# 18 of 22 MLP up units as Strassen's seven half-size products, the first conv tap on ScalarE

## The chip, the core and the metric

The kernel runs on one core of one Trainium2 chip. TensorE (PE) multiplies, VectorE (DVE), ScalarE (ACT) and GpSimd (POOL) work on tiles in SBUF, DVE and ACT also on PSUM, and SyncE (SP) issues the loads. The metric is the device time of one execution in microseconds; lower is better.

## The reference

Two layers of a decoder trunk over 512 tokens of width 1024, all in f32. Each layer has a token mixer, a cross-attention and a gated MLP, each between two RMS norms. The change is in the MLP alone:

```python
def conv_ffn(h, w_up, conv_w, conv_b, w_down):
    u = h @ w_up
    a, b = u[..., :D_FF], u[..., D_FF:]
    a = lax.conv_general_dilated(a, conv_w[:, None, :].astype(a.dtype), window_strides=(1,),
                                 padding=[(CONV_WIDTH - 1, 0)], dimension_numbers=('NWC', 'WIO', 'NWC'),
                                 feature_group_count=D_FF) + conv_b
    return (jax.nn.gelu(a) * b) @ w_down
```

with `D_FF` = 2816 and a convolution over three tokens, causal, channel by channel.

## The kernel before

**Precision.** Every large product runs in three passes on `float32r` operands: an f32 value is split into a high part (a copy to `float32r`) and a low part (the value less the high part), and the helper `three` issues low x high, high x low and high x high into one PSUM bank. Activations stand as `a_hi` and `a_lo`, 128 partitions x 8 chunks of the width x 512 tokens.

**Weights as a stream of units.** A layer reads 70 units of 1 MB. The up projection is units 36 to 57 (`U_UP` = 36), 22 of them, each 1024 x 256 columns: even ones for the value `a`, odd ones for the gate `b`. A unit is loaded by SP into one of two places of `raw`; ACT makes its high part in two halves of 128x1024 (L937, in `cast_halves`), POOL its low part in two halves (L795, `low_half`), and both stand in rings of two places, `w_hi` and `w_lo`. Unit u may be cast when an earlier unit has been used by PE (`unit_used`), and the low part waits for the high part.

**The up projection on PE.** The first pair of units (36 and 37) runs in halves of 256 tokens, from its own tiles `up_hi` and `up_lo`, between the transposes that still make `a_hi` and `a_lo`. From unit 38 on `cols_gemm` takes each unit in two column blocks of 128: for each 8 chunks x 3 matmuls with 512 tokens as the moving side, so 48 matmuls a unit, into two banks. Eight banks hold two pairs.

**Behind it.** With f one of 22 column blocks of 128 (`NF` = 22), DVE multiplies a bank by the third tap (`tensor_scalar`, L1687) and adds the two shifted taps (`scalar_tensor_tensor`, L1688 and L1689) into `conv`; ACT takes gelu of it into `gel` (L1244); DVE multiplies `gel` with the gate's bank into `gT` (`gate`, L1676). `gT` is then split for the down projection: high by ACT (`g_parts`), low by DVE (`g_rest`, L1670). Three of these splits stand within the up projection, the others behind it.

**Order.** Every engine runs its instructions in the order in which the code issues them, with semaphores between the engines. The order is written out by hand, one block for each engine; nothing is moved by a scheduler.

## Time and profile before

| | us |
|---|---|
| median of three runs (1682.21 to 1682.44) | 1682.44 |
| span of the profiled execution, first to last instruction | 1680.4 |
| PE busy | 1666.1 |
| POOL busy | 841.7 |
| ACT busy | 725.6 |
| DVE busy | 655.7 |

The page gives the profiled execution's span and no other time of it; what lies around the span is the difference to the runs, 2.0 us. Engines work side by side, so busy times don't add up. An instruction's duration runs from its start to its end; neighbours on an engine can overlap by some tens of nanoseconds, and a matmul's duration is longer than the distance to the next one. In a row, `[2.53 <-PE banks L1732]` is the engine's idle time before the instruction, and what ended it.

### The profile page before, as it was taken

What the parts mean: (1) busy time and instruction counts of PE and PEld (TensorE: products, weight loads), DVE (VectorE), ACT (ScalarE), POOL (GpSimd) and SP (SyncE); (2) the same over time, 40 slices, a digit from 0 to 9 for tenths busy, and PEclk for the clock granted to TensorE, in tenths of its full rate; (3) what the DMA queues carried; (4) which work ended last, traced back from release to release, by engine and by line L of the source; (5) the groups of instructions that cost most, each with busy time, mean ns of one, the idle gap of its engine ahead of it and who ended that gap; (6) DMA issues with size and microseconds to landing.
All of it is one profiled execution on the core that took longest, in us unless ns stands there. A gap on an engine that the chain in (4) does not pass through costs nothing.

```text
span 1680.4 us, 23253 instructions
## 1 busy us (share of the span) xinstructions
PE 1666.1 (99%) x9217; PEld 1366.6 (81%) x9217; DVE 655.7 (39%) x1423; ACT 725.6 (43%) x1386; POOL 841.7 (50%) x553
## 2 busy tenths in 40 slices
PE   9999999999999999999999999999999999999998
PEld 7888776888898888888888887768888988888886
DVE  3454665163272222311233456652442622232113
ACT  6326777363361222232362367764543522222322
POOL 4447667463443444445623567665634344443552
PEclk9999999999999999999999999999999999999999
DMA  6234111242232223232323340122413223332322
GB/s 227 76 96 137 51 27 52 80 146 75 64 99 96 85 95 100 76 125 100 110 93 100 93 139 27 26 53 87 163 50 109 81 75 101 100 101 75 106 95 75
DMA packets 101191, 154.15 MB, mean 92 GB/s; under 512 B 4396, under 2 KB 76380, under 8 KB 101084
## 3 DMA queue, kind: packets, MB, share of 16 engines
q1 hardware_dynamic: 98572, 147.16, 26.9%
q10 hardware_dynamic: 2512, 5.51, 0.9%
...
## 4 chain that ended last, share of the span: by engine, by line
PE 95%; ACT 1%; issue 1%; DVE 1%; POOL 1%; DVEq 0%; ACTq 0%; POOLq 0%
PE banks L1730 27%; PE banks L1732 27%; PE banks L1731 27%; PE banks L2045 4%; PE banks L2098 4%; PE banks L2074 4%; PE banks L1858 1%; PE banks L1774 1%; DVE proj L1559 1%; PE banks L2094 0%; PE banks L2242 0%; PE banks L1762 0%; POOL w_lo L795 0%; ACT w_hi L937 0%; ACT rows L906 0%
## 5 line engine op out<-in xcount | busy, mean ns | idle before, releaser
L795 POOL TENSOR_TENSOR w_lo<-raw,w_hi 128x1024 fp32r<-128x1024 f32 (+2 forms) x262 | 629.1, 2421 | 656.2 <-ACT w_hi L937 643.5
L937 ACT ACTIVATE w_hi<-raw 128x1024 fp32r<-128x1024 f32 (+2 forms) x264 | 259.8, 1028 | 643.4 <-PE banks L1732 635.5
L1730 PE MATMUL banks<-w_hi,a_lo 128*128 128x512 f32 (+1 forms) x864 | 332.5, 385 | 0.1
L1732 PE MATMUL banks<-w_hi,a_hi 128*128 128x512 f32 (+1 forms) x864 | 330.1, 382 | 0.0
L1731 PE MATMUL banks<-w_lo,a_hi 128*128 128x512 f32 (+1 forms) x864 | 330.0, 382 | 0.0
L1730 PE MATMUL banks<-a_hi,w_lo 128*128 128x512 f32 x768 | 299.6, 390 | 0.0
L1732 PE MATMUL banks<-a_hi,w_hi 128*128 128x512 f32 x768 | 298.9, 389 | 0.0
L1731 PE MATMUL banks<-a_lo,w_hi 128*128 128x512 f32 x768 | 298.8, 389 | 0.0
L1730 PEld LDWEIGHTS banks<-w_hi,a_lo 128*128 128x128 f32 x864 | 162.3, 188 | 32.8 <-issue 1.7
L1732 PEld LDWEIGHTS banks<-w_hi,a_hi 128*128 128x128 f32 x864 | 162.2, 188 | 31.3
L1731 PEld LDWEIGHTS banks<-w_lo,a_hi 128*128 128x128 f32 x864 | 162.3, 188 | 30.6
L1732 PEld LDWEIGHTS banks<-a_hi,w_hi 128*128 128x128 f32 x768 | 144.1, 188 | 30.0
L1731 PEld LDWEIGHTS banks<-a_lo,w_hi 128*128 128x128 f32 x768 | 144.2, 188 | 29.8
L1730 PEld LDWEIGHTS banks<-a_hi,w_lo 128*128 128x128 f32 x768 | 144.2, 188 | 29.3
L1687 DVE TENSOR_SCALAR conv<-banks,vecs 128x512 f32<-128x512 f32 x44 | 33.0, 749 | 224.8 <-PE banks L1732 224.8
L1545 DVE CUSTOM_DVE_ANT_0 banks<-banks,causal 128x128 f32<-128x128 f32 (+3 forms) x160 | 75.5, 512 | 40.2 <-PE banks L2045 40.2
L1670 DVE TENSOR_TENSOR a_lo<-gT,a_hi 128x1024 fp32r<-128x1024 f32 x18 | 28.6, 1592 | 153.3 <-ACT a_hi L1237 153.3
L805 POOL TENSOR_SCALAR proj<-proj,rden,gates 128x128 f32<-128x128 f32 (+3 forms) x128 | 76.4, 608 | 22.9 <-DVE rden L1563 22.5
L1093 ACT ACTIVATE proj<-banks,neg_max 128x128 f32<-128x128 f32 (+3 forms) x144 | 74.6, 526 | 7.3 <-DVE neg_max L1545 7.3
L2098 PE MATMUL banks<-probT,proj 128*64 128x128 f32 x960 | 73.6, 283 | 0.2
L2074 PEld LDWEIGHTS banks<-ident,proj 128*128 128x128 f32 x440 | 46.7, 140 | 32.8 <-issue 28.7
L2074 PE MATMUL banks<-ident,proj 128*128 128x128 f32 x440 | 67.8, 284 | 0.0
...
## 6 DMA issues: line engine op xcount, KB each, us to landing
raw<-in_ffn_w_up SPq DMA_DIRECT2D x44, 1024.0 KB, 5.1
raw<-in_ffn_w_down SPq DMA_DIRECT2D x20, 1024.0 KB, 4.9
raw<-in_w_in SPq DMA_DIRECT2D x19, 1024.0 KB, 5.1
raw<-in_x_wk SPq DMA_DIRECT2D x8, 1024.0 KB, 5.3
raw<-in_x_wv SPq DMA_DIRECT2D x8, 1024.0 KB, 4.9
raw<-in_x_wq SPq DMA_DIRECT2D x8, 1024.0 KB, 5.2
raw<-in_x_wo SPq DMA_DIRECT2D x8, 1024.0 KB, 5.0
raw<-in_cmp_wk SPq DMA_DIRECT2D x4, 1024.0 KB, 5.5
```

The costliest lines, as they stand in the source:

```text
L795: inc(pool.tensor_tensor(lo_half(u, half), raw_half(u, half), hi_half(u, half).bitcast(F32), ALU.subtract), lo_made, n)
L805: inc(pool.tensor_scalar(p, p, r, gate_of(i, hp), ALU.mult, ALU.mult), scaled_pool)
L937: inc(act.activation(hi_half(u, half), raw_half(u, half), ACT.Copy), hi_made)
L1093: inc(act.activation(probs(i, hp), s_bank(i, hp, item_keys(i), key_at(i)), ACT.Exp, scale=-1.0, bias=stat(neg_max, i, hp), accum_out=stat( ...
L1545: inc(dve.tensor_tensor_reduce(x, x, causal[:, S - n:S], -1.0, 3.0e38, ALU.add, ALU.min, stat(neg_max, i, hp)), maxed)
L1687: link(dve.tensor_scalar(cv, src, wcol(2), None, ALU.mult))
L1730: pe.matmul(dst, st_lo, mv_hi, start=first, stop=False)
L1731: pe.matmul(dst, st_hi, mv_lo, start=False, stop=False)
L1732: return pe.matmul(dst, st_hi, mv_hi, start=False, stop=last)
L2045: ins = pe.matmul(s_bank(i, hp, n + extra, key_at(i) - extra), qT[half, m, P * t:P * t + P], keys(row, n, extra)[half], start=True, stop=True)
L2074: ins = pe.transpose(bank(4 + hp, P, P * k), probs(i, hp)[:, P * k:P * k + P], ident[:])
L2098: ins = pe.matmul(bank(6, P, P * t)[half], proj[:, k, col:col + HD], pT(i)[:, kg, P * k:P * k + P], start=kind != "win" and t == 0 and k = ...
```

## The change

Units 40 to 57, 18 of the 22 (w = 0 to 17), are no longer a plain product. The weight unit (1024 x 256) is cut into quarters of 512 x 128, the activations into quarters of 4 chunks x 256 tokens, and the product is made by Strassen's scheme (Winograd's form) from seven products of sums of quarters. The weight sides are called `11`, `12`, `22` (quarters as they are) and `s1` to `s4` (sums). Per unit:

- DVE makes `s1`, `s2`, `s4`, `s3` from `raw` (128x512 each, to `w_sum` and `s4_sum`), and the low part of `22`.
- ACT makes seven high parts of 128x512, POOL six low parts of 128x512. They stand in `w_hi` and `w_lo` as eight places of 512 (`HELD`), seven per unit. POOL starts the low part of `s2` only when the sum `s4` is done.
- PE runs seven products of 12 matmuls with 256 tokens, into quarter-unit results of 256 columns in four banks, in the order `11`, then `22` of the unit before, `s2`, `s1`, `12`, `s3`, `s4`. The product `12` waits until ACT has copied the result of `11` (`keep_1`), `s3` for `keep_16`, `s4` for `keep_15`, and `22` for `make_22`.
- DVE adds the products up: `keep_16`, `keep_15`, `make_22`, `make_12`, `make_21`, each 128x256 with one input in PSUM and one in SBUF.
- The value's results now go to `gT`, in SBUF. The third tap is an ACT operation from there (`tap`), and the other two read `gT` and `conv`, both in SBUF. The gate still reads PSUM.

Once per layer the sums of the activations' quarters are made: seven operations of 128x1024 on DVE (`token_sums`), three on POOL (`token_sum_3`), then four high parts on ACT (`token_high`) and four low parts. Units 36 to 39 stay as they were, and so does the down projection. SP's loads wait for `piece_lo` of `12` and `part_22_lo` in place of `lo_made`.

```diff
+U_SEVEN, SEVENS = 40, 18
+HELD = 8
...
+PARTS = ("11", "s2", "s1", "12", "s3", "s4")
+HI_PARTS = ("11", "s1", "s2", "12", "s3", "s4")
+SUMS = ("s1", "s2", "s4", "s3")
...
+        def half_bank(w, name):
+            return bank(4 * (w % 2) + ("c11", "c12", "c21", "c22").index(name), 256)
...
+                def token_sum_3():
...
+                    pool.tensor_tensor(tok_sum[2][:], hi, other_hi, ALU.subtract)
+                    inc(pool.tensor_tensor(tok_spare[1][:], lo, other_lo, ALU.subtract), tok_3_part)
+                    pool.wait_ge(tok_3_part.sem, tok_3_part.at(l, 1))
+                    inc(pool.tensor_tensor(tok_sum[2][:], tok_sum[2][:], tok_spare[1][:], ALU.add), tok_3_summed)
+                    pool.wait_ge(tok_hi_made.sem, tok_hi_made.at(l, 3))
+                    inc(pool.tensor_tensor(tok_lo[2][:], tok_sum[2][:], tok_hi[2][:].bitcast(F32), ALU.subtract), tok_3_lo_made)
+                def part_low(w, part):
...
+                    pool.wait_ge(piece_hi.sem, piece_hi.at(l, nth(HI_PARTS, w, part)))
+                    hi, lo = part_of(w_hi, w, part), part_of(w_lo, w, part)
...
+                    if part in ("s1", "s2"):
+                        pool.wait_ge(part_summed.sem, part_summed.at(l, nth(SUMS, w, part) + 1))
+                    inc(pool.tensor_tensor(lo, src, hi.bitcast(F32), ALU.subtract), piece_lo)
...
+                        for w in range(SEVENS):
+                            for part in PARTS:
+                                part_low(w, part)
...
+                    inc(act.activation(conv[:, f % 3, :], gT[:, f, :], ACT.Copy, scale=vecs[:, 108 + f:109 + f]), tapped)
...
+                token_high(0)
+                token_high(1)
+                gelu_of(0)
+                gelu_of(1)
+                token_high(2)
+                gelu_of(2)
+                for part in HI_PARTS[:4]:
+                    part_high(0, part)
+                gelu_of(3)
+                for part in HI_PARTS[4:]:
+                    part_high(0, part)
+                token_high(3)
+                for w in range(SEVENS):
+                    after_value, more = w % 2 == 1, w + 1 < SEVENS
+                    if after_value:
+                        tap(w - 1, 0)
+                    keep_first(w)
+                    part_high(w, "22")
+                    if more:
+                        part_high(w + 1, "11")
+                    if after_value:
+                        tap(w - 1, 1)
+                    if more:
+                        for part in ("s1", "s2", "12"):
+                            part_high(w + 1, part)
+                    if after_value:
+                        gelu_of(column(w, 0))
+                    if more:
+                        part_high(w + 1, "s3")
+                    if after_value:
+                        gelu_of(column(w, 1))
+                    else:
+                        make_11(w)
+                    if more:
+                        part_high(w + 1, "s4")
+                    if w in (10, 12, 14):
+                        g_parts((w - 10) // 2)
...
+                def conv_taps(f):
+                    jp, b = divmod(f, 2)
+                    src = bank(up_bank(jp, 0) + b) if jp < 2 else gT[:, f, :]
+                    cv = conv[:, f % 3, :]
...
+                    if jp < 2:
...
+                    else:
+                        dve.wait_ge(tapped.sem, tapped.at(l, f - 3))
+                    link(dve.scalar_tensor_tensor(cv[:, 1:S], src[:, 0:S - 1], wcol(1), cv[:, 1:S], ALU.mult, ALU.add))
+                    inc(dve.scalar_tensor_tensor(cv[:, 2:S], src[:, 0:S - 2], wcol(0), cv[:, 2:S], ALU.mult, ALU.add), conved)
...
+                def token_sums():
+                    dve.wait_ge(aT_hi.sem, aT_hi.at(l, 40))
+                    dve.wait_ge(aT_lo.sem, aT_lo.at(l, 40))
...
+                    dve.tensor_tensor(tok_sum[0][:], part(a_hi, 0, 1), part(a_hi, 0, 0), ALU.subtract)
+                    link(dve.tensor_tensor(spare, part(a_lo, 0, 1), part(a_lo, 0, 0), ALU.subtract))
+                    inc(dve.tensor_tensor(tok_sum[0][:], tok_sum[0][:], spare, ALU.add), tok_summed)
+                    for n, i, j in ((1, 1, 1), (3, 1, 0)):
...
+                        link(dve.tensor_tensor(tok_sum[n][:], part(a_hi, i, j), before[:], ALU.subtract))
+                        inc(dve.tensor_tensor(tok_sum[n][:], tok_sum[n][:], part(a_lo, i, j), ALU.add), tok_summed)
...
+                    if part == "s1":
+                        dve.wait_ge(raw_landed[u % RING], landed(l, u))
+                        ins = dve.tensor_tensor(dst, quarter(u, 0, 1), quarter(u, 1, 1), ALU.add)
+                    elif part == "s2":
+                        dve.wait_ge(part_summed.sem, part_summed.at(l, nth(SUMS, w, "s1")))
+                        ins = dve.tensor_tensor(dst, s1, quarter(u, 0, 0), ALU.subtract)
+                    elif part == "s4":
+                        dve.wait_ge(part_summed.sem, part_summed.at(l, nth(SUMS, w, "s2")))
+                        ins = dve.tensor_tensor(dst, quarter(u, 1, 0), s2, ALU.subtract)
+                    else:
+                        ins = dve.tensor_tensor(dst, quarter(u, 0, 0), quarter(u, 0, 1), ALU.subtract)
...
+                def keep_sixth(w):
+                    wait_spent(dve, l, w, "s2")
+                    dve.wait_ge(kept_1.sem, kept_1.at(l, w + 1))
+                    inc(dve.tensor_tensor(keep_16[:], half_bank(w, "c21"), keep_1[:, w % 2, :], ALU.add), kept_16)
...
+                def make_22(w):
+                    wait_spent(dve, l, w, "s3")
+                    dve.wait_ge(kept_15.sem, kept_15.at(l, w + 1))
+                    inc(dve.tensor_tensor(tokens_done(w, "c22"), half_bank(w, "c21"), keep_15[:], ALU.add), made_22)
...
+                token_sums()
+                conv_taps(0)
+                token_low(0)
+                token_low(1)
+                conv_taps(1)
+                gate(0)
+                gate(1)
+                conv_taps(2)
+                for part in SUMS[:3]:
+                    part_sum(0, part)
+                conv_taps(3)
+                part_sum(0, "s3")
+                gate(2)
+                gate(3)
+                for w in range(SEVENS):
+                    if w:
+                        make_12(w - 1)
+                        columns(w - 1, 0)
+                        make_21(w - 1)
+                    part_22_low(w)
+                    if w == 0:
+                        dve.wait_ge(tok_hi_made.sem, tok_hi_made.at(l, 4))
+                        inc(dve.tensor_tensor(tok_lo[3], tok_sum[3][:], tok_hi[3].bitcast(F32), ALU.subtract), tok_lo_made)
+                    keep_sixth(w)
+                    if w + 1 < SEVENS:
+                        part_sum(w + 1, "s1")
+                        part_sum(w + 1, "s2")
+                    keep_fifth(w)
+                    if w + 1 < SEVENS:
+                        part_sum(w + 1, "s4")
+                        part_sum(w + 1, "s3")
+                    if w:
+                        columns(w - 1, 1)
+                    make_22(w)
+                    if w in (10, 12, 14):
+                        g_rest((w - 10) // 2)
+                make_12(SEVENS - 1)
+                columns(SEVENS - 1, 0)
+                make_21(SEVENS - 1)
+                columns(SEVENS - 1, 1)
...
-                for jp in range(1, 11):
-                    if jp >= 2:
-                        pe.wait_ge(gT_done.sem, gT_done.at(l, 2 * (jp - 2) + 2))
-                    cols_gemm(U_UP + 2 * jp, up_bank(jp, 0), up_psum)
-                    if jp == 9:
-                        pe.wait_ge(gT_done.sem, gT_done.at(l, 2 * 8 + 2))
-                    cols_gemm(U_UP + 2 * jp + 1, up_bank(jp, 1), up_psum)
...
+                def product(w, part, name, mv_hi, mv_lo, first=False):
+                    st_hi, st_lo = part_of(w_hi, w, part), part_of(w_lo, w, part)
+                    for k in range(4):
+                        ins = three(half_bank(w, name), st_hi[:, k, :], st_lo[:, k, :], mv_hi[:, k, :], mv_lo[:, k, :],
+                                    first and k == 0, k == 3, True)
+                    inc(ins, unit_used if part == "22" else part_spent)
...
+                for w in range(SEVENS):
+                    wait_banks(w, "c11")
+                    pe.wait_ge(piece_lo.sem, piece_lo.at(l, nth(PARTS, w, "11")))
+                    product(w, "11", "c11", tokens_of(a_hi, 0, 0), tokens_of(a_lo, 0, 0), True)
+                    if w:
+                        product_4(w - 1)
...
+                    pe.wait_ge(piece_lo.sem, piece_lo.at(l, nth(PARTS, w, "s2")))
+                    wait_banks(w, "c21")
+                    product(w, "s2", "c21", tok_hi[1], tok_lo[1], True)
+                    pe.wait_ge(piece_lo.sem, piece_lo.at(l, nth(PARTS, w, "s1")))
+                    wait_banks(w, "c12")
+                    product(w, "s1", "c12", tok_hi[0], tok_lo[0], True)
+                    pe.wait_ge(piece_lo.sem, piece_lo.at(l, nth(PARTS, w, "12")))
+                    pe.wait_ge(kept_1.sem, kept_1.at(l, w + 1))
+                    product(w, "12", "c11", tokens_of(a_hi, 1, 0), tokens_of(a_lo, 1, 0))
+                    pe.wait_ge(piece_lo.sem, piece_lo.at(l, nth(PARTS, w, "s3")))
+                    pe.wait_ge(kept_16.sem, kept_16.at(l, w + 1))
...
+                    product(w, "s3", "c21", tok_hi[2], tok_lo[2])
+                    pe.wait_ge(piece_lo.sem, piece_lo.at(l, nth(PARTS, w, "s4")))
+                    pe.wait_ge(kept_15.sem, kept_15.at(l, w + 1))
+                    product(w, "s4", "c12", tokens_of(a_hi, 1, 1), tokens_of(a_lo, 1, 1))
+                product_4(SEVENS - 1)
```

On DVE, in the steady state of the up projection, before: taps of one column block from a bank, the gate, one split.

```order
L1687 TENSOR_SCALAR conv<-banks,vecs 128x512
L1688 SCALAR_TENSOR_TENSOR conv<-banks,vecs,conv 128x511
L1689 SCALAR_TENSOR_TENSOR conv<-banks,vecs,conv 128x510
L1676 TENSOR_TENSOR gT<-gel,banks 128x512
L1687 TENSOR_SCALAR conv<-banks,vecs 128x512
L1688 SCALAR_TENSOR_TENSOR conv<-banks,vecs,conv 128x511
L1689 SCALAR_TENSOR_TENSOR conv<-banks,vecs,conv 128x510
L1676 TENSOR_TENSOR gT<-gel,banks 128x512
```

The same place now, one unit: the unit w is odd here, so the taps are those of the value before it (`keep_84`, `keep_123` and `keep_109` are `keep_16`, `keep_15` and `keep_1`).

```order
L1995 TENSOR_TENSOR w_lo<-raw,w_hi 128x512
L2001 TENSOR_TENSOR keep_84<-banks,keep_109 128x256
L1981 TENSOR_TENSOR w_sum<-raw 128x512
L1984 TENSOR_TENSOR w_sum<-w_sum,raw 128x512
L2006 TENSOR_TENSOR keep_123<-banks,keep_109 128x256
L1987 TENSOR_TENSOR s_sum<-raw,w_sum 128x512
L1989 TENSOR_TENSOR w_sum<-raw 128x512
L1946 SCALAR_TENSOR_TENSOR conv<-gT,vecs,conv 128x511
L1947 SCALAR_TENSOR_TENSOR conv<-gT,vecs,conv 128x510
L2012 TENSOR_TENSOR banks<-banks,keep_123 128x256
L2018 TENSOR_TENSOR banks<-banks,keep_84 128x256
L1931 TENSOR_TENSOR gT<-gel,banks 128x512
```

Between the taps stand now the low part of `22`, the four sums and the additions; the taps read `gT` where they read `banks`.

On POOL, from the first up unit on, before:

```order
L795 TENSOR_TENSOR up_lo_70<-raw,up_hi_68 128x1024 x2
L795 TENSOR_TENSOR up_lo_71<-raw,up_hi_69 128x1024 x2
L795 TENSOR_TENSOR w_lo<-raw,w_hi 128x1024 x40
L795 TENSOR_TENSOR w_lo<-raw,w_hi 128x512 x4
L795 TENSOR_TENSOR w_lo<-raw,w_hi 128x1024 x20
```

And now, up to the parts of the first seven-product unit:

```order
L921 TENSOR_TENSOR w_lo<-raw,w_hi 128x1024 x4
L980 TENSOR_TENSOR tok_sum_113<-a_hi 128x1024
L981 TENSOR_TENSOR tok_spare_122<-a_lo 128x1024
L983 TENSOR_TENSOR tok_sum_113<-tok_sum_113,tok_spare_122 128x1024
L985 TENSOR_TENSOR tok_lo_120<-tok_sum_113,tok_hi_117 128x1024
L1000 TENSOR_TENSOR w_lo<-raw,w_hi 128x512
L1000 TENSOR_TENSOR w_lo<-w_sum,w_hi 128x512 x2
L1000 TENSOR_TENSOR w_lo<-raw,w_hi 128x512
L1000 TENSOR_TENSOR w_lo<-w_sum,w_hi 128x512
L1000 TENSOR_TENSOR w_lo<-s_sum,w_hi 128x512
L1000 TENSOR_TENSOR w_lo<-raw,w_hi 128x512
```

POOL's 36 low parts of the 18 units are replaced by four operations on tokens and 108 low parts of half the size.

At the start of the up projection DVE had, behind the last `a_lo`:

```order
L1370 SCALAR_TENSOR_TENSOR a_lo<-banks,vecs,a_hi 128x256 x8
L1687 TENSOR_SCALAR conv<-banks,vecs 128x512
L1688 SCALAR_TENSOR_TENSOR conv<-banks,vecs,conv 128x511
L1689 SCALAR_TENSOR_TENSOR conv<-banks,vecs,conv 128x510
L1687 TENSOR_SCALAR conv<-banks,vecs 128x512
L1688 SCALAR_TENSOR_TENSOR conv<-banks,vecs,conv 128x511
L1689 SCALAR_TENSOR_TENSOR conv<-banks,vecs,conv 128x510
L1676 TENSOR_TENSOR gT<-gel,banks 128x512
```

and has now:

```order
L1619 SCALAR_TENSOR_TENSOR a_lo<-banks,vecs,a_hi 128x256 x8
L1955 TENSOR_TENSOR tok_sum_111<-a_hi 128x1024
L1956 TENSOR_TENSOR tok_spare_121<-a_lo 128x1024
L1957 TENSOR_TENSOR tok_sum_111<-tok_sum_111,tok_spare_121 128x1024
L1961 TENSOR_TENSOR tok_sum_112<-a_hi,tok_sum_111 128x1024
L1962 TENSOR_TENSOR tok_sum_112<-tok_sum_112,a_lo 128x1024
L1961 TENSOR_TENSOR tok_sum_114<-a_hi,tok_sum_112 128x1024
L1962 TENSOR_TENSOR tok_sum_114<-tok_sum_114,a_lo 128x1024
L1943 TENSOR_SCALAR conv<-banks,vecs 128x512
L1946 SCALAR_TENSOR_TENSOR conv<-banks,vecs,conv 128x511
L1947 SCALAR_TENSOR_TENSOR conv<-banks,vecs,conv 128x510
L1967 TENSOR_TENSOR tok_lo_118<-tok_sum_111,tok_hi_115 128x1024
```

The seven operations of `token_sums` stand ahead of the first tap, and two token low parts ahead of the second block's taps.

## Rows read from the trace of the kernel before

**Rows 1.** The page: span, busy time of each engine, the chain that ended last.
```profile
span 1680.4 us, 23253 instructions
...
PE 1666.1 (99%) x9217; PEld 1366.6 (81%) x9217; DVE 655.7 (39%) x1423; ACT 725.6 (43%) x1386; POOL 841.7 (50%) x553
...
PE 95%; ACT 1%; issue 1%; DVE 1%; POOL 1%; DVEq 0%; ACTq 0%; POOLq 0%
```

**Rows 2.** Windows over the first layer's up-projection stretch.
```profile
core 0: us, PE busy (x) PEld busy (x) DVE busy (x) ACT busy (x) POOL busy (x), PEclk, DMA share, GB/s
503.60:721.10 217.50, 217.50 (x961) 180.11 (x961) 62.45 (x83) 52.94 (x62) 89.97 (x39) 1.00 0.29 93
```

**Rows 3.** Timeline of PE: 512-column matmuls, nine intervals apart (start, duration in us).
```profile
1343.54 0.39 PE L1730 MATMUL banks<-a_hi,w_lo 128*128 128x512 f32 x1
...
1345.58 0.39 PE L1730 MATMUL banks<-a_hi,w_lo 128*128 128x512 f32 x1
```

**Rows 4.** Timeline of PE: 256-column matmuls, first and last of 66.
```profile
481.36 0.28 PE L1730 MATMUL banks<-a_hi,up_lo 128*128 128x256 f32 x1
...
489.07 0.28 PE L1732 MATMUL banks<-a_hi,up_hi 128*128 128x256 f32 x1
```

**Rows 5.** Timeline: POOL low parts of 512, a DVE tap under them.
```profile
711.25 2.55 POOL L795 TENSOR_TENSOR w_lo<-raw,w_hi 128x512 fp32r<-128x512 f32 x2 [5.70 <-ACT w_hi L937]
...
711.27 0.75 DVE L1688 SCALAR_TENSOR_TENSOR conv<-banks,vecs,conv 128x511 f32<-128x511 f32 x1
```

**Rows 6.** Groups of instructions, shapes apart (busy us, mean ns | idle before).
```profile
L1676 DVE TENSOR_TENSOR gT<-gel,banks 128x512 f32<-128x512 f32 x44 | 30.0, 681 | 55.4 <-PE banks L1732 55.4
...
L1631 DVE TENSOR_TENSOR xpT_lo<-banks,xpT_hi 128x256 fp32r<-128x256 f32 x32 | 13.4, 419 | 3.0 <-ACT xpT_hi L1197 0.8
...
L937 ACT ACTIVATE w_hi<-raw 128x512 fp32r<-128x512 f32 x8 | 4.6, 620 | 16.5 <-PE banks L1732 16.5
```

**Rows 7.** Timeline from 722: DVE `a_lo` of 1024 free and contested, POOL free and contested.
```profile
722.52 1.22 DVE L1670 TENSOR_TENSOR a_lo<-gT,a_hi 128x1024 fp32r<-128x1024 f32 x1 [0.40 <-ACT a_hi L1237]
...
733.44 2.41 POOL L795 TENSOR_TENSOR w_lo<-raw,w_hi 128x1024 fp32r<-128x1024 f32 x1 [0.68 <-ACT w_hi L937]
...
735.29 1.64 DVE L1670 TENSOR_TENSOR a_lo<-gT,a_hi 128x1024 fp32r<-128x1024 f32 x1 [11.55 <-ACT a_hi L1237]
...
735.80 3.37 POOL L795 TENSOR_TENSOR w_lo<-raw,w_hi 128x1024 fp32r<-128x1024 f32 x1
```

**Rows 8.** Timeline near 627: a DVE operation of 512 between two of POOL.
```profile
626.67 0.92 DVE L1670 TENSOR_TENSOR first_lo<-gT,first_hi 128x512 fp32r<-128x512 f32 x1 [5.76 <-ACT first_hi L1237]
...
627.00 2.85 POOL L795 TENSOR_TENSOR w_lo<-raw,w_hi 128x1024 fp32r<-128x1024 f32 x1
```

**Rows 9.** Timeline: DVE operations that came after POOL had begun.
```profile
914.16 0.42 DVE L1300 TENSOR_TENSOR rope_tmp<-proj,cos_t 128x256 f32<-128x256 f32 x1
914.50 2.62 DVE L1301 TENSOR_TENSOR rope_tmp<-proj,sin_t 128x256 f32<-128x256 f32 x1
...
914.18 2.67 POOL L795 TENSOR_TENSOR w_lo<-raw,w_hi 128x1024 fp32r<-128x1024 f32 x1 [7.88 <-ACT w_hi L937]
...
1023.73 1.81 POOL L817 TENSOR_TENSOR proj<-proj 128x768 f32<-128x768 f32 x1 [0.89 <-DVE proj L1559]
...
1024.14 2.48 DVE L1559 TENSOR_TENSOR_SCAN proj<-relu_z,proj 128x512 f32<-128x512 f32 x1
```

**Rows 10.** Timeline: last matmul of a unit's first half, and the tap behind it.
```profile
514.22 0.39 PE L1732 MATMUL banks<-a_hi,w_hi 128*128 128x512 f32 x1
...
514.64 0.75 DVE L1687 TENSOR_SCALAR conv<-banks,vecs 128x512 f32<-128x512 f32 x1 [2.53 <-PE banks L1732]
```

**Rows 11.** Timeline at the start of the stretch: DVE and POOL.
```profile
491.70 2.78 DVE L1370 SCALAR_TENSOR_TENSOR a_lo<-banks,vecs,a_hi 128x256 fp32r<-128x256 f32 x5 [0.32 <-ACT a_hi L982]
...
494.99 9.45 POOL L795 TENSOR_TENSOR w_lo<-raw,w_hi 128x1024 fp32r<-128x1024 f32 x4 [15.83 <-ACT w_hi L937]
```

**Rows 12.** The page's DMA issues: KB each, us to landing.
```profile
raw<-in_ffn_w_up SPq DMA_DIRECT2D x44, 1024.0 KB, 5.1
```

More of the change, by code:

```diff
@@ L205, in up_bank, with place_of, part_at, nth @@
 def up_bank(jp, half):
-    if jp < 9:
-        return 2 * (jp % 2) + 4 * half
-    return ((2, 0), (6, 4))[jp - 9][half]
+    return 2 * jp + 4 * half
+PARTS = ("11", "s2", "s1", "12", "s3", "s4")
+HI_PARTS = ("11", "s1", "s2", "12", "s3", "s4")
+SUMS = ("s1", "s2", "s4", "s3")
+def place_of(w, part):
+    if part == "22":
+        return 7 * w + 7 if w < SEVENS - 1 else 7 * w + 6
+    i = PARTS.index(part)
+    return i if w == 0 else 7 * w - 1 + (i + 1 if i else 0)
+def part_at(place):
+    for w in range(SEVENS):
+        for part in PARTS + ("22",):
+            if place_of(w, part) == place:
+                return w, part
+def nth(names, w, part):
+    return len(names) * w + names.index(part) + 1
+def plain_before(n):
+    if n > 2 * UNITS:
+        return 2 * (UNITS - SEVENS) + plain_before(n - 2 * UNITS)
+    return n if n <= 2 * U_SEVEN else max(2 * U_SEVEN, n - 2 * SEVENS)
 def row_broadcast(vec, l):
@@ L313, in build @@
         stage = view("stage", [P, 5, P], F32, W)
+        end = region(4096)
+        keep_1 = view("keep_1", [P, 2, 256], F32, W + 28672)
+        s4_sum = view("s4_sum", [P, 4, P], F32, W + 30720)
+        tok_sum = [view(f"tok_sum{i}", [P, 4, 256], F32, W + 6 * S * 4 + 4096 * i) for i in range(4)]
+        tok_hi = [view(f"tok_hi{i}", [P, 4, 256], F32R, at) for i, at in enumerate((R, R + 8192, M + 4096))] + [a_hi[:, 0:4, 256:512]]
+        tok_lo = [view(f"tok_lo{i}", [P, 4, 256], F32R, at) for i, at in enumerate((R + 4096, R + 12288, end))] + [a_lo[:, 0:4, 256:512]]
+        tok_spare = [view(f"tok_spare{i}", [P, 4, 256], F32, at) for i, at in enumerate((R + 4096, end))]
+        keep_15 = new("keep_15", [P, 256])
         ident = new("ident", [P, P])
@@ L1248, in _ @@
+                cast_to(U_DOWN + 1)
                 act.preload_act_table_set("natural_log_exp_and_others")
@@ new lines, in make_21, with columns @@
+                def make_21(w):
+                    wait_spent(dve, l, w, "22")
+                    inc(dve.tensor_tensor(tokens_done(w, "c21"), half_bank(w, "c21"), keep_1[:, w % 2, :], ALU.add), made_21)
+                def columns(w, b):
+                    (gate if w % 2 else conv_taps)(column(w, b))
+                token_sums()
[5 more added lines that the diff above has]
+                gate(1)
@@ L1726, in _, with three @@
             pe.wait_ge(pro_const, 1)
-            def three(dst, st_hi, st_lo, mv_hi, mv_lo, first, last):
-                pe.matmul(dst, st_lo, mv_hi, start=first, stop=False)
-                pe.matmul(dst, st_hi, mv_lo, start=False, stop=False)
-                return pe.matmul(dst, st_hi, mv_hi, start=False, stop=last)
+            def three(dst, st_hi, st_lo, mv_hi, mv_lo, first, last, shared=False):
+                pe.matmul(dst, st_lo, mv_hi, start=first, stop=False, skip_group_check=shared)
+                pe.matmul(dst, st_hi, mv_lo, start=False, stop=False, skip_group_check=shared)
+                return pe.matmul(dst, st_hi, mv_hi, start=False, stop=last, skip_group_check=shared)
             def first_pieces(at_l):
@@ new lines, in _ @@
+                hi, lo = unit(U_UP + 3)
+                for k in range(KD):
+                    if k == 4:
+                        rest(U_UP + 3)
+                    for m in range(2):
+                        mm = slice(P * m, P * m + P)
+                        ins = three(bank(up_bank(1, 1) + m), hi[:, k, mm], lo[:, k, mm], a_hi[:, k, :], a_lo[:, k, :], k == 0, k == KD - 1)
+                        if k == KD - 1:
+                            inc(ins, (up_psum, unit_used)[m])
+                    if k in (1, 3, 5):
+                        inc(ins, part_spent)
```

221 lines of the change are left out of this document (189 added, 32 removed).

## Prediction

> **What bounds the kernel now.** I read the page first: of a span of 1680.4 us TensorE is busy 1666.1 us, and the chain that ended last is 95% PE [rows 1]. Then the first layer's up projection from unit 38 on, by windows: in its 217.5 us PE is busy for all 217.5 us at a granted clock of 1.00 (the 2.4 GHz level), while DVE works 62.45 us, ACT 52.94 and POOL about 90 [rows 2]. So the stretch is matmuls in a row and nothing else; 961 of them in 217.5 us are 0.2263 us each. The timeline says the same: nine intervals between 1343.54 and 1345.58 us, 0.2267 us each for 512 columns [rows 3]. A matmul's own 0.39 us is its passage; the distance between starts is what it costs. One up unit is 48 such matmuls: 10.88 us. The 18 units that change are 195.8 us of each layer.
>
> **What the change takes from PE.** A unit becomes 7 products of 12 matmuls with 256 columns: 84 x 256 = 21,504 columns in place of 48 x 512 = 24,576. The kernel already runs such a shape, with fresh weights for every matmul, in the first two up units: 65 intervals from 481.36 to 489.07 us are 0.1186 us each [rows 4], a little more than half of 0.2267. 84 x 0.1186 = 9.96 us, so PE could save 0.92 us a unit, 33 us for 36 units. That is all there is to win.
>
> **What it adds.** Per unit, in steady state:
> POOL: six low parts of 128x512 in place of two of 128x1024. Two such operations took 2.55 us together, the second starting 1.26 us after the first [rows 5]: 6 x 1.26 = 7.6 us (before 4.8).
> ACT: seven high parts at 0.62 us [rows 6], one copy of a product, and per two units a `make_11`, two taps and two gelus: some 6.5 us. It has room.
> DVE: four weight sums and one low part (128x512, both inputs in SBUF), five additions from PSUM (128x256), and on average two `scalar_tensor_tensor` and one gate. With 0.61 us from start to start for the sums (0.69 by the rows 1.22 us at 1024 and 0.68 for the gate at 512, less an overlap of 0.08), 0.36 for an addition (0.42 less 0.06), 0.79 for a tap (0.75 [rows 5] and its wait) and 0.62 for a gate [rows 6, 7], two units are 6.1 + 3.6 + 3.2 + 1.2 = 14.1 us of DVE, against 19.9 us of PE. By busy time alone everything fits under PE.
>
> **What busy time hides: DVE and POOL shut each other out.** A low part that took 2.41 us alone took 3.37 us when a DVE `tensor_tensor` with two SBUF inputs (1.64 us instead of its free 1.22) came between: POOL lost 0.96 us to 1024 elements [rows 7]. With a DVE operation of 512 elements it took 2.85: 0.44 us lost [rows 8]. The other way round, a DVE operation of 256 elements (0.42 us elsewhere) that came just after a POOL operation of 2.67 us had begun took 2.62 us: it waited for all of it [rows 9]. This is a turn-taking, not a sharing. An operation with one input in PSUM does not take part: a tap from a bank ran in 0.75 us under a POOL operation [rows 5]. Today this costs nothing, since the few contested operations lie under PE.
>
> In the new code seven DVE operations per unit have both inputs in SBUF: `s1`, `s2`, `s4`, `s3`, the low part of `22`, and two taps, which now read `gT` and `conv` where they read a bank. For `tensor_tensor` the rows above price it. For `scalar_tensor_tensor` from SBUF no row exists; the nearest is the scan, also with two SBUF inputs, which took 2.48 us and ended after POOL's operation of 1.81 us that had begun before it, so it waited too [rows 9]. I take it as contested; the lower bound is that it is not.
>
> The Trainium skill has this as a rule ("SBUF — State Buffer", Who interferes with whom): a VectorE instruction with two SBUF inputs contends with a GpSimd one that reads SBUF, and the later one blocks fully. The trace agrees, with 2.62 us for 0.42 [rows 9], for the five `tensor_tensor`; of the two taps it shows nothing. By the rule the turns of a unit are the 10.6 us below; if the taps were outside it, they would be 9.8, which is rival (a).
>
> So the shared resource is occupied per unit for 6 x 1.26 + 7 x 0.44 = 10.6 us. That is already more than PE's 9.96, and only 0.24 under today's 10.88.
>
> **The order makes it worse.** Both engines keep to the order written. A DVE turn of 1024 elements lasted from POOL's end at 735.85 us to 736.93, 1.07 us, and cost POOL 0.96 [rows 7]: POOL hides 0.1 of it. So I hold 0.53 us for a DVE turn of 512 and 1.16 (1.26 less 0.1) for a POOL turn, and walk one unit from the end of the sum `s4` (time 0). DVE: `s3` to 0.53. POOL: low `s2` to 1.69. DVE: tap to 2.22. POOL: low `s1` to 3.38. DVE: second tap to 3.91. POOL: `12` to 5.1, then `s3` to 6.3; DVE meanwhile `make_22` (4.4), `make_12`, gate. PE may start the product `22` only after `make_22`, at 4.5, and ends it at 5.9; DVE sees a product some 0.4 us after its last matmul began (514.22 to 514.64 [rows 10]), so `make_21` ends at 6.5, low `22` at 7.1, POOL's `s4` at 8.3. `keep_16` waits for PE's `s2` and ends at 7.9. Then `s1` to 8.8, POOL's `11` to 10.0, `s2` to 10.5, `keep_15` 11.0, `s4` 11.6. The next unit, with the gate before `make_22` and the taps after `make_12` and an ACT tap, comes to 11.3 the same way. I take 11.4 us, 0.5 over today's unit. PE then waits 1.4 us in each.
>
> **The start of the stretch.** `token_sums` puts seven DVE operations of 1024 elements at 494.5 us, where DVE's last `a_lo` ends, and POOL has four low parts of 2.4 us from 494.99 on [rows 11]. In turns of 1.07 and 2.26 us, with POOL's own `token_sum_3` behind, the seventh ends at about 515.8 (unhindered about 502.5, seven times 1.15). Only then come both first taps, `token_low` twice, and gelu 0 and 1 on ACT, which stand ahead of `token_high(2)`: 524.7. POOL's `tok_lo` waits for that, and every weight part is queued behind it: low `11` ends at about 529.3. PE is ready for the first product at 503.6 (where the stretch begins [rows 2]) + 2 x 10.88 = 525.4. It waits 4 us, and 1.5 more behind `token_high(3)`, so I give the first seven-product unit 15.5 us. The last has no next unit to prepare: 10.0. The three `g_rest` in units 10, 12 and 14, contested like the sums (0.53, 0.53, 1.07 us and a POOL turn for some), now lie on DVE's full queue: 4 us a layer.
>
> **Sum.** Per layer 15.5 + 16 x 11.4 + 10.0 + 4 = 211.9 us, against 195.8: +16.1, for two layers +32. The profiled execution's span becomes 1712.6. Its page gives no time but the span; the median of the runs is 2.0 us over it, and I add that: 1714.6 us. I cost the other edits at nothing: a raw unit now has about one unit's time, 11 us, from the place being free to its first use, against 5.1 to land [rows 12]; without that cover it would be 5 us a unit.
>
> **Rivals.** (a) PE stays the bound, faster. This needs the turns to add up to less than 9.96 us a unit, which allows 5.5 contested DVE operations, not 7. If `scalar_tensor_tensor` from SBUF is not contested, there are 5: 7.56 + 2.2 = 9.8 us. For it: nothing in the trace shows one; against: the scan. Units of 9.96 us with the start's 5.5 us and 1 for the rest give 2 x (18 x 9.96 + 6.5 - 195.8) = -20: 1662 us. Chance 0.08.
> (b) The turns pack perfectly, no other wait: 10.7 us a unit. 2 x (15.5 + 17 x 10.7 - 195.8) = +3: 1686 us. For it: the engines' waits can shift until the holes fill; against: `keep_16` and `make_21` wait for PE in the middle of DVE's queue. Chance 0.12; it falls half on no change.
> (c) DVE waits a POOL turn at every contested operation, also where my walk lets it slip in first: 0.9 us more per unit, 12.3. 2 x (16.1 + 16 x 0.9) = +61: 1743 us. Chance 0.10.
> (d) My forecast, DVE and POOL in turns at 11.0 to 11.9 us a unit: 1700 to 1731. Chance 0.70.
>
> **Numbers.** The range runs from just under the slow side of (b) to between (d) and (c): 1688 to 1740. A change within 0.2%, 3.4 us, can't be told from none here. Faster is (a) and a tail of (b), 0.10; same is part of (b), 0.06; slower the rest, 0.84.
>
> **What will show it.** The 256-column matmuls 0.119 us apart, but PE idle 1 to 2 us per unit, before the products `22`, `s2` or `s4`; the sums and taps on DVE with means well over 0.69 and 0.75 us (1.2 and more) while additions from PSUM stay at 0.42; POOL's low parts at 1.5 us or more instead of 1.29; a wait of 4 us or more before the first product. I am wrong if taps from `gT` run in 0.75 us under POOL operations, or if PE has no idle time between units.

## The result, and the profile after

The changed kernel takes 1735.17 us, the median of four runs (1734.11 to 1736.33), against 1682.35 us before on the same chip: a ratio of 1.0314 (95% interval 1.0299 to 1.0329), 53 us slower. The forecast was 1714 us, 32 us slower, in a range of 1688 to 1740.

The page of the changed kernel: the span, busy times, the chain that ended last, and two groups (busy us, mean ns | idle before, releaser).

```profile
span 1734.6 us, 27411 instructions
...
PE 1671.5 (96%) x10513; PEld 1431.3 (83%) x10513; DVE 951.1 (55%) x1767; ACT 846.7 (49%) x1664; POOL 1033.6 (60%) x705
...
PE 75%; DVE 15%; issue 6%; ACT 3%; POOL 2%; DVEq 0%; ACTq 0%; POOLq 0%
...
L1000 POOL TENSOR_TENSOR w_lo<-w_sum,w_hi 128x512 fp32r<-128x512 f32 x108 | 165.3, 1544 | 97.5 <-DVE s_sum L1987 97.5
...
L1000 POOL TENSOR_TENSOR w_lo<-raw,w_hi 128x512 fp32r<-128x512 f32 x72 | 119.1, 1654 | 2.1 <-ACT w_hi L1434 1.8
```

Beside [rows 1], PE has fallen from 95% of the chain to 75%, and DVE, which was 1% of it, is 15%. No engine is busy longer than PE. POOL's low parts of 512 take 1.54 and 1.65 us, where two had taken 2.55 together [rows 5].

The stretch of the 18 units in the first layer, on PE's timeline (start, duration). It runs from the last plain matmul to the first of the down projection, 222.4 us after PE could have begun (about 525.2), against 18 x 10.88 = 195.8 before. The second layer shows the same, so the stretch holds the whole loss (2 x 26.6 = 53).

```profile
524.77 0.39 PE L2107 MATMUL banks<-a_hi,w_hi 128*128 128x512 f32 x1
529.04 0.55 PE L2105 MATMUL banks<-a_hi,w_lo 128*128 128x256 f32 x1 [3.88 <-POOL w_lo L1000]
...
539.52 0.36 PE L2105 MATMUL banks<-tok_hi,w_lo 128*128 128x256 f32 x1 [2.13 <-issue]
...
552.60 0.35 PE L2105 MATMUL banks<-a_hi,w_lo 128*128 128x256 f32 x1 [1.00 <-DVE keep L2006]
...
557.52 0.36 PE L2105 MATMUL banks<-a_hi,w_lo 128*128 128x256 f32 x1 [1.82 <-DVE banks L2012]
...
581.27 0.36 PE L2105 MATMUL banks<-a_hi,w_lo 128*128 128x256 f32 x1 [1.82 <-DVE banks L2012]
...
747.58 0.47 PE L2105 MATMUL banks<-w_hi,first_lo 128*128 128x512 f32 x1
```

The rows at 557.52 and 581.27 are the same place two units apart: 23.75 us, of which PE needs 20.2 (168 matmuls 0.12 us apart). What DVE does in the first of these two units:

```profile
553.58 1.78 DVE L1946 SCALAR_TENSOR_TENSOR conv<-gT,vecs,conv 128x511 f32<-128x511 f32 x1
555.40 1.64 DVE L1947 SCALAR_TENSOR_TENSOR conv<-gT,vecs,conv 128x510 f32<-128x510 f32 x1
556.96 0.42 DVE L2012 TENSOR_TENSOR banks<-banks,keep 128x256 f32<-128x256 f32 x1
...
559.83 0.43 DVE L2023 TENSOR_TENSOR banks<-banks,keep 128x256 f32<-128x256 f32 x1 [1.30 <-PE banks L2107]
560.17 1.04 DVE L1995 TENSOR_TENSOR w_lo<-raw,w_hi 128x512 fp32r<-128x512 f32 x1
562.16 0.42 DVE L2001 TENSOR_TENSOR keep<-banks,keep 128x256 f32<-128x256 f32 x1 [0.95 <-PE banks L2107]
562.50 0.68 DVE L1981 TENSOR_TENSOR w_sum<-raw 128x512 f32<-128x512 f32 x1
```

The two taps from SBUF hold DVE for 3.4 us where 1.5 would do. `make_22` (L2012) ends 4.3 us after the sum `s4` (at 553.06), and PE's product `22` waits for it. Then DVE waits for PE twice. The sum at 562.50 meets no POOL operation and takes its free 0.68.

That is so for most sums. The groups of DVE and one wait of POOL, from 553 to 720 us (busy us, mean ns; the wait: total, times, longest):

```profile
L1947 DVE SCALAR_TENSOR_TENSOR conv<-gT,vecs,conv 128x510 f32<-128x510 f32 x14 | 23.1, 1651 | 0.5
L1995 DVE TENSOR_TENSOR w_lo<-raw,w_hi 128x512 fp32r<-128x512 f32 x14 | 17.8, 1274 | 0.0
L1981 DVE TENSOR_TENSOR w_sum<-raw 128x512 f32<-128x512 f32 x13 | 11.9, 915 | 0.0
L1987 DVE TENSOR_TENSOR s_sum<-raw,w_sum 128x512 f32<-128x512 f32 x14 | 9.5, 681 | 0.0
...
POOL w_lo L1000 <- DVE s_sum L1987: 37.5, 14, 3.4
```

Of the seven operations that could meet POOL in a unit, the two taps and the low part of `22` carry most of the waiting and `s1` a part (915 ns); `s2`, `s4` and `s3` run at 0.68 to 0.76 us on average: POOL stands idle for 2.7 us in each unit (37.5 us in 14), until the sum `s4` is made, and most of these sums fall into that time.

One thing was not in the forecast. After these waits the granted clock drops; windows of the same unit (the length comes first, then PE's busy time with its matmuls; the clock is the third number from the end):

```profile
559.00:562.00 3.00, 3.00 (x17) 3.00 (x17) 1.38 (x2) 0.62 (x2) 3.00 (x3) 0.55 0.02 5
562.00:565.00 3.00, 3.00 (x28) 3.00 (x27) 2.65 (x5) 1.62 (x3) 0.36 (x1) 1.00 0.86 268
```

At a granted clock of 0.55 (near the 1.2 GHz level) 17 matmuls start in 3 us, at 1.00 (2.4 GHz) 28.

### The profile page after: what moved, and what is told of

The parts are those of the page before. It is cut to its first block, busy times and chain, and to the rows that moved or that the text cites. A ratio compares the mean times of both kernels' runs of the same rounds, so it can differ in the third digit from the quotient of the medians.

```text
span 1734.6 us, 27411 instructions
## 1 busy us (share of the span) xinstructions
PE 1671.5 (96%) x10513; PEld 1431.3 (83%) x10513; DVE 951.1 (55%) x1767; ACT 846.7 (49%) x1664; POOL 1033.6 (60%) x705
## 4 chain that ended last, share of the span: by engine, by line
PE 75%; DVE 15%; issue 6%; ACT 3%; POOL 2%; DVEq 0%; ACTq 0%; POOLq 0%
PE banks L2105 20%; PE banks L2107 20%; PE banks L2106 20%; PE banks L2420 4%; PE banks L2473 4%; PE banks L2449 4%; DVE conv L1946 3%; DVE w_sum L1981 1%; PE banks L2233 1%; DVE w_sum L1989 1%; DVE w_sum L1984 1%; DVE w_lo L1995 1%; DVE tok_sum L1961 1%; DVE tok_sum L1962 1%; DVE s_sum L1987 1%
## 5 line engine op out<-in xcount | busy, mean ns | idle before, releaser
L921 POOL TENSOR_TENSOR w_lo<-raw,w_hi 128x1024 fp32r<-128x1024 f32 (+2 forms) x190 | 463.4, 2459 | 406.7 <-ACT w_hi L1104 394.0
L2105 PE MATMUL banks<-a_hi,w_lo 128*128 128x256 f32 (+1 forms) x768 | 246.1, 320 | 36.5 <-DVE banks L2012 26.4
L2107 PE MATMUL banks<-a_hi,w_hi 128*128 128x256 f32 (+1 forms) x768 | 243.1, 317 | 0.0
L2106 PE MATMUL banks<-a_lo,w_hi 128*128 128x256 f32 (+1 forms) x768 | 242.7, 316 | 0.0
L1000 POOL TENSOR_TENSOR w_lo<-w_sum,w_hi 128x512 fp32r<-128x512 f32 x108 | 165.3, 1544 | 97.5 <-DVE s_sum L1987 97.5
L2105 PE MATMUL banks<-tok_hi,w_lo 128*128 128x256 f32 x432 | 129.6, 300 | 11.9 <-DVE keep L2001 6.9
L2106 PE MATMUL banks<-tok_lo,w_hi 128*128 128x256 f32 x432 | 128.3, 297 | 0.0
L2107 PE MATMUL banks<-tok_hi,w_hi 128*128 128x256 f32 x432 | 128.0, 296 | 0.0
L1000 POOL TENSOR_TENSOR w_lo<-raw,w_hi 128x512 fp32r<-128x512 f32 x72 | 119.1, 1654 | 2.1 <-ACT w_hi L1434 1.8
L2105 PEld LDWEIGHTS banks<-tok_hi,w_lo 128*128 128x128 f32 x432 | 90.2, 209 | 13.5 <-issue 13.5
```

Of the source, the lines that this page charges most:

```text
L921: inc(pool.tensor_tensor(lo_half(u, half), raw_half(u, half), hi_half(u, half).bitcast(F32), ALU.subtract), lo_made, n)
L1000: inc(pool.tensor_tensor(lo, src, hi.bitcast(F32), ALU.subtract), piece_lo)
L2105: pe.matmul(dst, st_lo, mv_hi, start=first, stop=False, skip_group_check=shared)
L2106: pe.matmul(dst, st_hi, mv_lo, start=False, stop=False, skip_group_check=shared)
L2107: return pe.matmul(dst, st_hi, mv_hi, start=False, stop=last, skip_group_check=shared)
```

## The experiments

All against the kernel before, at 1682.2 to 1682.4 us on the same chip as each run.

| run | us | ratio to before, 95% interval |
|---|---|---|
| changed kernel | 1735.2 | 1.0314 (1.0299 to 1.0329) |
| pool_writes_only | 1666.3 | 0.9905 (0.9884 to 0.9926) |
| pe_filler | 1735.3 | 1.0316 (1.0297 to 1.0334) |
| taps_from_psum | 1689.5 | 1.0044 (1.0028 to 1.0060) |
| low12_on_dve | 1723.7 | 1.0247 (1.0231 to 1.0263) |
| first_tap_on_dve | 1767.6 | 1.0514 (1.0499 to 1.0528) |
| start_reordered | 1731.6 | 1.0291 (1.0277 to 1.0305) |
| psum_low12 | 1677.1 | 0.9968 (0.9956 to 0.9980) |
| psum_low12_start | 1676.0 | 0.9964 (0.9950 to 0.9978) |
| psum_low2_start | 1673.3 | 0.9950 (0.9937 to 0.9962) |
| psum_low2_start2 | 1674.2 | 0.9949 (0.9936 to 0.9963) |

**Is it the turn-taking, or the order and DVE's own work?** Each of POOL's low parts is replaced, in its place in the order, by three fills, which read nothing. They take 1.37 us together (527, 527 and 313 ns), where a low part that nothing holds up takes 1.26; the low parts are then zero.

```diff
-                    inc(pool.tensor_tensor(lo, src, hi.bitcast(F32), ALU.subtract), piece_lo)
...
+                    for i in range(2):
+                        inc(pool.memset(lo, 0.0), filled)
+                        pool.wait_ge(filled.sem, filled.at(l, n + i + 1))
+                    inc(pool.memset(lo[:, 0:2, :], 0.0), piece_lo)
```

> The changed kernel, but POOL's 216 low parts of the seven-product units are replaced by three fills of the same place (512, 512 and 256 elements, about 1.35 us together, as long as the real operation), which write SBUF and read nothing; the low parts are then zero. If turn-taking between DVE and POOL is the loss: DVE's sums and taps fall to 0.69 and 0.75 us, PE no longer idles at `22`, its clock stays at 1.00, a unit takes 10.0 to 10.3 us (changed kernel: 11.9), and the time is 1665 to 1680 us. If it is instead the order itself, DVE waiting for PE and ACT in the middle of its queue: a unit stays at 11.4 us or more, 1715 us or more.

It took 1666.3 us (two runs). Two groups of DVE from 553 to 720 us in its trace (mean ns after the comma), and a window of all engines:

```profile
L1953 DVE SCALAR_TENSOR_TENSOR conv<-gT,vecs,conv 128x510 f32<-128x510 f32 x16 | 12.0, 750 | 0.6
...
L1987 DVE TENSOR_TENSOR w_sum<-raw 128x512 f32<-128x512 f32 x15 | 10.2, 682 | 0.0
```

```profile
545.00:570.00 25.00, 25.00 (x211) 25.00 (x210) 19.03 (x34) 15.19 (x27) 20.44 (x47) 1.00 0.39 128
```

The second tap falls from 1651 to 750 ns, the sum `s1` (L1987 here) from 915 to 682, and PE runs without a gap. The order is the same, so in the steady units the order alone costs nothing; what costs is POOL's reading while DVE reads two operands from SBUF. PE's units now stand 10.08 us apart, and the 3.8 us wait at the start remains, since the token sums still meet POOL.

**Does the drop of the clock cost time?** Fourteen matmuls into an unused half bank ahead of the wait for `make_22` in odd units keep PE at work:

```diff
+                    if w % 2:
+                        for _ in range(14):
+                            pe.matmul(bank(3, 256, 256), a_hi[:, 0, 0:P], a_hi[:, 0, 0:256], start=True, stop=True)
                     pe.wait_ge(made_22.sem, made_22.at(l, w + 1))
```

> The changed kernel with 14 matmuls more (256 columns, into an unused half bank, 1.7 us) on PE before its wait for `make_22` of every odd unit, where it idled 1.8 us and the granted clock then fell, so that about 15 matmuls stood 0.213 us apart in place of 0.119. If that fall, 1.4 us in every second unit, is part of the path: the clock stays at 1.00, 1690 to 1715 us. If DVE and POOL in turns bind alone and the slow matmuls lie beside their work: 1731 us or more, no change.

It took 1735.3 us, the same. A window of its trace: the clock stays up.

```profile
559.00:562.00 3.00, 3.00 (x27) 3.00 (x26) 2.42 (x4) 1.03 (x2) 3.00 (x3) 1.00 0.00 0
```

The next rows are the first tap of the following pair, in the changed kernel and then in this one; the tap before them stood at 553.58 and at 553.96.

```profile
577.32 1.79 DVE L1946 SCALAR_TENSOR_TENSOR conv<-gT,vecs,conv 128x511 f32<-128x511 f32 x1
```

```profile
577.26 1.79 DVE L1946 SCALAR_TENSOR_TENSOR conv<-gT,vecs,conv 128x511 f32<-128x511 f32 x1
```

So this pair takes 23.30 us in place of 23.74, and fourteen units take 166.9 us in place of 169.8: the lower clock is worth 0.2 us a unit, 2.9 us a layer. The filler gives 0.4 of them back in the first two units and 1.7 at the last, where it has nothing to hide behind, which leaves 0.8 a layer; the medians can't tell that. The drop follows from the wait and is not its cause: the lower clock holds some 6 of the 53 us here, and a little at the start.

**Taps that read PSUM.** The value's results stay in their banks, and the taps read them there. A column block lies in two half banks, so each tap gets a piece of 1 or 2 columns more. Five contested DVE operations a unit are left, the case that rival (a) prices. (ACT's copy `make_11` into `gT` also goes, and DVE's additions write to the banks.)

```diff
-            if w % 2:
-                return half_bank(w, name)
-            at = 256 * (name in ("c12", "c22"))
-            return gT[:, column(w, name in ("c21", "c22")), at:at + 256]
+            return half_bank(w, name)
```

> The changed kernel, but the value's results stay in their PSUM banks as the gate's do; ACT's tap and DVE's two taps read them there (four short pieces more per column block across the bank's edge), so that DVE has five operations per unit with two SBUF inputs, not seven. By turns a unit is 6 x 1.26 + 5 x 0.44 = 9.8 us, under PE's 9.96: taps at 0.75 us, units of 10.2 to 10.8 us, 1670 to 1695 us. If the taps were not contested, or the order is the loss: no gain, 1730 us or more (DVE has slightly more to do).

It took 1689.5 us, 45.6 less than the changed kernel and within the range. Groups of DVE from 553 to 720 us:

```profile
L1988 DVE TENSOR_TENSOR w_sum<-raw 128x512 f32<-128x512 f32 x15 | 21.6, 1442 | 0.0
L1991 DVE TENSOR_TENSOR w_sum<-w_sum,raw 128x512 f32<-128x512 f32 x15 | 21.3, 1419 | 1.9 <-DVE w_sum L1988 0.5
L2002 DVE TENSOR_TENSOR w_lo<-raw,w_hi 128x512 fp32r<-128x512 f32 x16 | 19.8, 1238 | 0.0
L1949 DVE SCALAR_TENSOR_TENSOR conv<-banks,vecs,conv 128x508 f32<-128x508 f32 x17 | 12.7, 747 | 0.6
```

The taps are free at 747 ns. The sums `s1` and `s2` and the low part of `22` now carry the waits. A pair takes 20.83 us, 10.4 a unit: by rival (a)'s sum of turns (9.8 us) PE should have been the bound, at 10.08, and it is not quite.

**One low part from POOL to DVE.** `12` in place of POOL's sixth turn of 1.26 us becomes a DVE turn of 0.5 (`MOVED` holds `12` alone).

```diff
                     make_22(w)
+                    if w + 1 < SEVENS and "12" in MOVED:
+                        moved_low(w + 1, "12")
```

> The changed kernel, but the low part of `12` is made by DVE behind `make_22` and not by POOL: DVE has 0.61 us more work per unit, POOL 1.26 less. By turns a unit is 5 x 1.26 + 8 x 0.44 = 9.8 us: units of 10.5 to 11.2 us, 1685 to 1710 us. If DVE's own work is the bound (it is the busiest helper), it is slower: 1735 + 34 x 0.6 = 1755 us.

It took 1723.7 us, 11.5 less: the right sign, so DVE's own work was not the limit, but short of the range. The waits of its trace from 553 to 720 us (total, times, longest) show what is left: PE still waits for `make_22` (L2032), behind the two contested taps.

```profile
PE banks L2129 <- DVE banks L2032: 12.5, 7, 2.0
```

**The second part of the change undone alone.** DVE makes the first tap from `gT`, and ACT none.

```diff
-                        dve.wait_ge(tapped.sem, tapped.at(l, f - 3))
...
+                        dve.wait_ge(gelued.sem, gelued.at(l, f - 2))
+                        link(dve.tensor_scalar(cv, src, wcol(2), None, ALU.mult))
```

> Undoes the second part of the change alone: the first tap of the 16 columns of a layer that the seven-product units make is a scaling by VectorE from the SBUF column again, and ScalarE does none. If VectorE's and GpSimd's work with their turns sets the pace (my theory), each of the 32 columns adds one VectorE operation of 0.5 to 0.75 us to it, less 0.43 us that VectorE now waits for ScalarE's tap on average: 1738 to 1759 us. Rival: VectorE has room enough (it is busy 176 us of 212) and the move to ScalarE was worth nothing: 1733 to 1737 us.

It took 1767.6 us, 32.5 more, 1.0 us a column block and over my range of 1738 to 1759. The group of DVE from 553 to 720 us:

```profile
L1937 DVE TENSOR_SCALAR conv<-gT,vecs 128x512 f32<-128x512 f32 x13 | 17.2, 1320 | 0.6
```

With one SBUF input and an SBUF output this operation takes 1320 ns on average, 469 to 1529 over the whole trace, where from a bank it took 750 [rows 10]: free it would be faster than from PSUM, but it meets POOL as well. In the first layer the one that met no POOL operation (at 758.44) took the 469. So the ScalarE tap, taken alone, is worth 32 us to this version.

**The start.** ACT's rounding of the third token sum and of the first quarter stand ahead of gelus, and DVE's sums of the first unit ahead of gates and taps:

```diff
+                token_high(2)
                 gelu_of(0)
+                part_high(0, "11")
                 gelu_of(1)
-                token_high(2)
...
+                for part in SUMS[:3]:
+                    part_sum(0, part)
+                conv_taps(2)
                 gate(0)
                 gate(1)
-                conv_taps(2)
-                for part in SUMS[:3]:
-                    part_sum(0, part)
```

> Same work as the changed kernel; only the order at the start of each layer's seven-product units differs: ScalarE rounds the third token sum and the first quarter ahead of the gelus of columns 0 to 2, and VectorE makes the sums s1, s2, s4 of the first unit ahead of the taps of column 2 and the gates of columns 0 and 1. In the changed kernel TensorE waits 3.9 us per layer for the first low part, which stands behind the token sums and behind that rounding (at 522.92). If the chain through the rounding is what is late (my theory), the wait of 3.9 us is mostly gone in both layers and the 2.1 us wait of the first unit's s3 shrinks: 1721 to 1729 us. Rival: the turns that the token sums take (VectorE's at 3.3 us each) are what is late, and moving the rounding does nothing: 1733 us or more.

It took 1731.6 us, 3.5 less: between my range (1721 to 1729) and the rival's (1733 or more). Its PE rows show the first wait gone and another in its place:

```profile
527.76 0.36 PE L2106 MATMUL banks<-tok_hi,w_lo 128*128 128x256 f32 x1 [1.04 <-DVE conv L1948]
...
534.20 0.55 PE L2106 MATMUL banks<-a_hi,w_lo 128*128 128x256 f32 x1 [3.33 <-ACT keep L1442]
```

**Together.**

> Three edits together: the value results stay in PSUM so that the taps read no two SBUF operands (alone 1689.5 us), the low part of quarter 12 is made by VectorE instead of GpSimd (alone 11.5 us less than the changed kernel), and the start in its new order. With the turn theory 5 GpSimd turns of 1.26 us and 6 contested VectorE operations of 0.44 us make 8.9 us a unit and VectorE's own work about 8.0, both under TensorE's 10.0: TensorE is the bound in the steady units, and 1655 to 1678 us comes out, under the kernel before. Rival: the two first edits take the same turns away and do not add up, or VectorE is over its limit: 1683 us or more.

> As the run before it, with the low part of quarter 11 on VectorE as well: 4 GpSimd turns of 1.26 us and 7 contested VectorE operations, 8.1 us a unit, VectorE's own work about 8.6 us. If the number of GpSimd turns is what still costs, it is 2 to 10 us under the run before it; if VectorE's queue (its order, in which a low part waits for ScalarE) now binds, it is the same or slower. 1655 to 1680 us.

> As the run with taps from PSUM, the low parts of 11 and 12 on VectorE and the start reordered (1673.3 us), with one more change of order at the start: ScalarE's gelu of column 3 stands behind the copy of the first product (keep_1) instead of ahead of it, and VectorE makes the taps of column 2 ahead of the sum s4 and the sum s3 ahead of the taps of column 3. In the trace of that run TensorE's steady units stand 10.08 us apart (nothing is left to gain there), and the stretch of 18 units takes 190.6 us, 9.1 over 18 x 10.08: 2.4 in the units with g_rest, 0.8 waiting for the taps of column 2, 3.3 waiting for keep_1, and 2.6 for the matmuls at the lower granted clock behind these waits. If ScalarE's queue is the cause of that wait and the wait is the cause of the lower clock, 3.3 to 6.5 us a layer come back: 1660 to 1667 us. If another wait takes its place: 1670 us or more.

> Taps from PSUM and the low part of quarter 12 on VectorE, without the new start (with it 1676.0 us; taps from PSUM alone 1689.5). It tells how the gain of 13.5 us splits. If the start's order is worth what it was worth alone (3.6 us) and the low part what it was worth alone (11.5 us): 1678 to 1681 us. If in a kernel whose steady units are near TensorE's bound the start shows in full (some 4 us a layer) and the low part only the rest: 1682 to 1686 us.

They took 1676.0, 1673.3, 1674.2 and 1677.1 us, in this order. The first two lie in their ranges; the third came out as its rival (another wait takes the place), and the fourth is under both of its ranges. Taps from PSUM with one low part moved is faster than the kernel before by 0.3%, with two low parts by 0.5%. The steady units of all four are 10.08 us apart. In the third (`psum_low2_start2`) the wait for `keep_1` went and these came:

```profile
528.61 0.36 PE L2143 MATMUL banks<-tok_hi,w_lo 128*128 128x256 f32 x1 [2.01 <-POOL w_lo L1012]
...
536.64 0.36 PE L2143 MATMUL banks<-tok_hi,w_lo 128*128 128x256 f32 x1 [3.24 <-issue]
```

The order of the start is worth 1 us in 1677 here, within the intervals. In the 1673.3 us run DVE is busy 37 of the 40 us from 505 to 545, and each new order moved PE's wait to another operation: a tap, `keep_1`, a low part. Against 1682.3 - 36 x 0.80 = 1653.5, where PE would lose nothing, the best run is 20 us over, 10 a layer. In its first layer some 7 lie in the first two units and 2.4 in those with `g_rest`. I did not take the start apart further; whether fewer token sums on DVE would win it stays open.

## Why the prediction was right, and where it was off

**The bound and what PE saves.** Right in kind. The size was a little off: I carried 0.1186 us from [rows 4], while the products run 0.12 apart, nine intervals in 1.08 us:

```profile
567.84 0.28 PE L2106 MATMUL banks<-a_lo,w_hi 128*128 128x256 f32 x1
...
568.92 0.28 PE L2106 MATMUL banks<-a_lo,w_hi 128*128 128x256 f32 x1
```

84 of them are 10.08 us, so 29 us could be won, not 33. In the runs with PE free of gaps the units are 10.08 us apart.

**DVE and POOL shut each other out.** Right, and shown: with POOL writing only, the loss of 53 us becomes a gain of 16. The assumption that had no row, that `scalar_tensor_tensor` from SBUF is contested, is right, at 1.78 and 1.64 us beside 0.75. That decided against rival (a)'s premise. The Trainium skill ("SBUF — State Buffer", Who interferes with whom) says that a VectorE instruction with two SBUF inputs contends with GpSimd's reads and not with its writes; both halves agree here, with 1651 and 750 ns for one tap.

**Sum of turns, then order.** I held the unit at 10.6 us by turns and 11.4 by the walk. Measured: 11.9, and 12.3 to 12.6 behind a `g_rest`. The walk is right to `make_22` (4.3 us, I had 4.4). The step that failed is the one behind it: I let `make_21` end at 6.5, the low part of `22` at 7.1 and `keep_16` at 7.9; in the trace they end at 7.2, 8.2 and 9.5 after the sum `s4`. With the filler they end at 6.6, 8.2 and 8.5: so the low part waits for a POOL operation in any case, and the lower clock adds the rest. Later sums meet an idle POOL and get part of it back: the next `s4` ends at 11.85, where I had 11.6. One of my signs did not come for that reason: I expected the sums at 1.2 us and more, and they took 0.68 to 0.92 on average, while the taps took 1.57 and 1.65. So not all seven operations took a turn, and the walk is near for a part by luck: it has the stretch to `keep_16` 1.6 us too short and the one from there to the next `s4` some 1.4 us too long (3.7 for 2.35). Fourteen units took 169.8 us (557.52 to 727.34) where I had 14 x 11.4 + 4 = 163.6.

**PE's wait per unit.** 1.4 forecast in each; it is 1.8 in every second, at `make_22` after taps, as I had said, and next to none in the others, but for 0.5 to 2.5 us behind a `g_rest`. The lower clock behind each wait of 1.8 costs about 1.5 us more on PE, for which I had no term.

**The start.** The first low part: its end was forecast at 529.3 us, PE starts at 529.04. The seventh token sum: 515.8 forecast, 515.5 measured. But the first two units took 32.3 us (525.2 to 557.52) where the sum gives 15.5 + 11.4 = 26.9. Behind the fourth token low part, and so behind `token_high(3)`, PE waits 2.1 us for `s3`, not 1.5; I did not see the wait of 1.0 for `s4`, nor that the matmuls behind the wait of 3.9 us would run at the lower clock, 40 in 7 us, where 58 would fit (2.2 us):

```profile
529.00:532.00 3.00, 2.96 (x14) 2.99 (x15) 2.93 (x5) 0.29 (x1) 2.41 (x2) 0.50 0.00 0
532.00:536.00 4.00, 4.00 (x26) 4.00 (x26) 2.23 (x4) 3.73 (x7) 4.00 (x4) 0.70 0.00 0
```

The last two units lost nothing, 20.2 us where the sum gives 11.4 + 10.0.

**The sum.** 222.4 us a layer, not 211.9: of the 10.5, 6.2 come from the fourteen steady units and 5.4 from the first two, less 1.2 in the last two. The mechanism held; the terms for a unit and the start were too small, both for want of what follows a wait.

**Rivals.** (a) and (b) are out. (a)'s condition was then made by hand, five contested operations: 1689.5 us and not 1662. A sum of turns 3% under PE's time did not make PE the bound here, where the order has waits both ways. (c) had 12.3 us a unit; the units stayed within (d)'s 11.0 to 11.9, and the total went 4 us over (d)'s 1731 by the start.
